# Forget term as one product of 64 rows, built on ScalarE; a gate sigmoid from exponentials and a logarithm; four modulation pieces moved ahead

## What is computed

```python
mod = c_act @ ada_w[layer] + ada_b[layer]          # shifts, scales, gates: 6 x 1024 for each layer
h = modulate(rms_norm(x, kv_norm_g), shift, scale)  # shared_kv
kvf = h @ kv_w                                      # k, v and 16 forget logits
dcum = cumsum(log_sigmoid(f_logit), axis=1)
...
qg = h @ w_qg                                       # fox_mixer, with h modulated by other vectors
q, gate = rms_norm(qg[..., :D]), sigmoid(qg[..., D:])
logits = (q @ k.T) * scale + dcum[t] - dcum[s]      # 16 heads of 64, causal
o = softmax(logits) @ v
y = (o * gate) @ w_o
```

## Time and profile before

| | |
|---|---|
| median of three runs | 1785.41 us (1780.71 to 1785.68) |
| profiled execution: its own time, its span | 1787.7 us, 1785.9 us |
| PE busy | 1735.7 us, 97% of the span |
| DVE, ACT busy | 1141.9 us (64%), 897.9 us (50%) |
| mean granted TensorE clock | 0.987 of full |
| DMA | 363.45 MB, mean 204 GB/s |

### The profile page before, as it was taken

The page is one execution under the profiler, slowest core; times in us unless marked ns, Lnnn a source line. Parts: engine busy times, 40 slices in busy tenths (PEclk is TensorE's granted clock), DMA queues, the critical chain, the costliest instruction groups (busy, mean ns, idle before and its releaser), DMA issues.

```text
span 1785.9 us, 22395 instructions
## 1 busy us (share of the span) xinstructions
PE 1735.7 (97%) x9104; PEld 1444.5 (81%) x9104; DVE 1141.9 (64%) x1588; ACT 897.9 (50%) x1282; POOL 7.7 (0%) x21
## 2 busy tenths in 40 slices
PE   8999999999999999999999989999999999999998
PEld 5898788888867888888888867888888889778887
DVE  3779978779666754565547967554655556675553
ACT  4645644465657444554444566444544445574432
POOL 0000000000000000000000000000000000000000
PEclk9999999999989999999999999999999999999999
DMA  9957677866615665555555324545554556345451
GB/s 385 379 227 295 238 306 294 305 244 230 258 72 189 235 222 179 200 191 181 176 201 183 119 71 177 183 171 188 204 186 175 192 205 224 111 149 181 170 195 47
DMA packets 54984, 363.45 MB, mean 204 GB/s; under 512 B 5841, under 2 KB 9041, under 8 KB 14690
## 3 DMA queue, kind: packets, MB, share of 16 engines
q1 hardware_dynamic: 53122, 351.47, 53.6%
q0 software_dynamic: 1760, 10.56, 1.5%
HBM read 360.96 MB, written 1.05 MB: 203 GB/s over the span
## 4 chain that ended last, share of the span: by engine, by line
PE 79%; DVE 10%; ACT 2%; issue 1%; DMA 0%; DVEq 0%; ACTq 0%
PE pp L633 76%; DVE low L1892 3%; PE pp L908 2%; DVE raw L1905 1%; PE pp L840 1%; DVE hf L2036 1%; PE pp L985 1%; ACT wh L1350 1%; DVE hl L1892 0%; DVE Sb L2187 0%; DVE sc L2288 0%; DVE x L1895 0%; DVE tb L1892 0%; DVE h L1892 0%; DVE top L2285 0%
## 5 line engine op out<-in xcount | busy, mean ns | idle before, releaser
L1892 DVE TENSOR_TENSOR low<-raw,wh 128x2048 fp32r<-128x2048 f32 (+3 forms) x346 | 638.8, 1861 | 367.9 <-ACT wh L1350 367.7
L1350 ACT ACTIVATE wh<-raw 128x2048 fp32r<-128x2048 f32 (+3 forms) x352 | 537.2, 1544 | 417.5 <-PE pp L633 288.1
L633 PE MATMUL pp<-wh,hh 128*128 128x512 f32 x1312 | 522.7, 398 | 7.4 <-ACT hh L1617 2.2
L633 PE MATMUL pp<-low,hh 128*128 128x512 f32 x1312 | 514.0, 392 | 1.8 <-DVE low L1892 1.6
L633 PE MATMUL pp<-wh,hl 128*128 128x512 f32 x1312 | 507.2, 392 | 3.7 <-DVE hl L1892 3.7
L633 PEld LDWEIGHTS pp<-wh,hh 128*128 128x128 f32 x1312 | 247.6, 189 | 65.3 <-issue 13.9
L633 PEld LDWEIGHTS pp<-wh,hl 128*128 128x128 f32 x1312 | 247.5, 189 | 57.6 <-DVE hl L1892 5.0
L633 PEld LDWEIGHTS pp<-low,hh 128*128 128x128 f32 x1312 | 248.0, 189 | 51.8 <-DVE low L1892 3.5
L633 PE MATMUL pp<-wh,hidh 128*128 128x512 f32 x592 | 232.0, 392 | 0.0
L633 PE MATMUL pp<-low,hidh 128*128 128x512 f32 x592 | 230.6, 389 | 0.3 <-DVE low L1892 0.3
L633 PE MATMUL pp<-wh,hidl 128*128 128x512 f32 x592 | 230.6, 389 | 0.0
(11 more groups left out here) (226 smaller groups left out, 1190.7 us busy)
## 6 DMA issues: line engine op xcount, KB each, us to landing
raw<-in_w SPq DMA_DIRECT2D x300, 1024.0 KB, 4.8
raw<-in_w SPq DMA_DIRECT2D x24, 768.0 KB, 4.3
raw<-in_w SPq DMA_DIRECT2D x13, 512.0 KB, 19.1
firstw<-in_w SPq DMA_DIRECT2D x6, 1024.0 KB, 14.8
gain<-in_w POOLq DMA_DIRECT2D x6, 512.0 KB, 4.8
bT<-in_rel POOLq DMA_DIRECT2D x1, 2048.0 KB, 12.0
cst<-in_csts POOLq DMA_DIRECT2D x1, 1029.0 KB, 7.2
xT<-in_xT SPq DMA_DIRECT2D x1, 1024.0 KB, 5.8
```

What stands on the lines that cost most here:

```text
L633: return e.matmul(out, lhsT, rhs, start=start, stop=stop, skip_group_check=True)
L1350: q.then_inc(e.activation(wh[j % NW][:, c], raw_of(i, kt * n)[:, c], ACT.Copy), s_wh, (j, part))
L1892: return e.tensor_tensor(out, a, b, op)
```

## The change

Four edits in one. First, the forget term: `dcum` is no longer split into two tiles; rows 32 to 63 and 96 to 127 of `dH` are overwritten with the rest (the rows hold copies of the same 16 logits), so hi and rest stand below each other in 64 rows, and each unit adds one fp32r product of 64 rows. The left side and eight right sides are built on ACT. Second, `h3` is built on ACT (`third_h`), in 16 activations of 128x128, and the transposes' PSUM banks are given back by ACT. Third, sigmoid(x) = exp(min(x,0) - ln(1 + exp(-|x|))): ACT does Abs, Exp, Ln and a last Exp, DVE does `gate_min` (out of the PSUM) and `gate_less`. No other table set is loaded. The PSUM area is free when the second `gate_min` has read. In the fill of attention, a step without work is added before `head_norm("q1")` and one before "own". Fourth, `marks`: by the 52nd piece 36 and not 32 ada pieces are mixed in, so that four more lie in the first feed-forward and none between `kv_v` and the second `kv_v`.

```diff
-    marks = [(0, 0), (6, 4), (18, 12), (20, 12), (52, 32), (56, 32), (72, 44), (78, 44), (88, 48)]
+    marks = [(0, 0), (6, 4), (18, 12), (20, 12), (52, 36), (61, 36), (70, 44), (78, 44), (88, 48)]
@@ tensor: s_h3 is signalled by third_h on ACT
+            if hv == 3:
+                return s_h3, ("hf", 3, m, c)
@@ tensor: attention, scores
-                            rr = slice(32 * (h % 4), 32 * (h % 4) + 32)
-                            for i in range(2):
-                                ins = mm(s_r.of((kind, "s", u["u"], s))[:, 0:nk], dL[i][rr, 128 * u["qb"]:128 * u["qb"] + 128],
-                                         dR[i][h // 4][rr, 0:nk], False, i == 1)
+                            rr = u["rows"]
+                            ins = mm(s_r.of((kind, "s", u["u"], s))[:, 0:nk], dL[rr, 128 * u["qb"]:128 * u["qb"] + 128],
+                                     dR[h // 2][rr, 0:nk], False, True)
@@ tensor: fill
                 yield from group("q1", 0, h(3), (s_side, ("qk", "q1")), fillp)
                 yield
+                yield
                 head_norm("q1", t_r)
                 yield "second"
-                yield from group("gate1", 0, h(3), (s_gate, ("gate", 1)), fillp)
+                yield from group("gate1", 0, h(3), (s_side, ("gate_min", 1, 1)), fillp)
+                yield
                 yield "own"
@@ scalar
-                q.then_inc(e.activation(gT[:, 4 * g:4 * g + 4, :], ring.of((("gate", "gate1")[g], 0)).tiles, ACT.Sigmoid),
-                           s_gate, ("gate", g))
-                log_tables()
+            def gate_log(g, ring):
+                ...
+                for n in range(2):
+                    t = slice(2 * n, 2 * n + 2)
+                    q.then_inc(e.activation(a[:, t, :], ring.of((("gate", "gate1")[g], 0)).tiles[:, t, :], ACT.Abs),
+                               s_sideact, ("gate_abs", g, n))
+                q.wait_ge(s_sideact, ("gate_abs", g, 1))
+                q.then_inc(e.activation(a, a, ACT.Exp, scale=-1.0), s_sideact, ("gate_exp", g))
+                q.wait_ge(s_sideact, ("gate_exp", g))
+                q.then_inc(e.activation(a, a, ACT.Ln, bias=1.0), s_sideact, ("gate_log", g))
+            def gate_sigmoid(g):
+                o = gT[:, 4 * g:4 * g + 4, :]
+                q.wait_ge(s_side, ("gate_less", g))
+                q.then_inc(e.activation(o, o, ACT.Exp), s_gate, ("gate", g))
@@ scalar: fill (gate_sigmoid(0) in q1's fourth step)
                 head_squares("q1", fillp)
                 yield
+                yield
                 head_roots("q1", t_r)
...
-                gate_sigmoid(1, fillp)
+                gate_log(1, fillp)
                 waiting("fox", 4, gT)
+                yield
                 yield "own"
+                gate_sigmoid(1)
@@ scalar: main order
+            def third_h(m):
+                ...                 # 2 x 4 activations 128x128, PSUM -> h3, scale and bias per row
+            def forget_sides():
+                ...                 # waits for the two "dD"
+                e.activation(dL[:, :], dH[:, :], ACT.Identity, bias=fc[:, 1:2], scale=fc[:, 0:1])
+                for j in range(8):
+                    ins = e.activation(dR[j][:, :], dH[:, :], ACT.Identity, bias=fc[:, 10 + j:11 + j], scale=fc[:, 2 + j:3 + j])
+                q.then_inc(ins, s_sideact, "dR")
             for g in range(2):
-                ahead.group("kv_k", g)
+                ahead.group("kv_k", g, between=lambda: third_h(g))
...
             values(("vv", 1), "kv_v", 1, vv[:, :, 512:1024])
-            ahead.group("q", 0)
+            forget_sides()
+            ahead.group("q", 0, upto=1)
             head_squares("q")
             ahead.first("gate", 0)
             head_roots("q")
-            gate_sigmoid(0, pairs)
+            gate_log(0, pairs)
@@ vector
+            def gate_min(g, ring):
+                ...                 # 2 x min(x, 0), PSUM -> gT, 128x512, each after its gate_abs
+            def gate_less(g):
+                ...                 # gT = gT - log, 128x1024
@@ vector: fill (gate_less(0) in q1's third step)
                 yield from ahead.steps("gate1", 0, "T")
+                gate_min(1, fillp)
                 for tile in range(4):
                     lo_of(4, tile, gT[:, tile, :])
+                yield
+                gate_less(1)
                 yield "own"
@@ vector: main order
-            ahead.group("kv_k", 0, between=lambda: h_parts(3, 0, *inputs_of("q")))
+            ahead.group("kv_k", 0)
-            ahead.group("kv_k", 1, between=lambda: h_parts(3, 1, *inputs_of("q")))
+            ahead.group("kv_k", 1)
-            q.then_inc(tt(dD[:, :], dT[:, :], dH[:, :], ALU.subtract), s_side, "dD")
-            q.wait_ge(s_side, "dD")
-            for i, d in enumerate((dH, dD)):
-                e.tensor_scalar(dL[i][:, :], d[:, :], fc[:, 0:1], fc[:, 1:2], ALU.mult, ALU.add)
-                for j in range(4):
-                    ins = e.tensor_scalar(dR[i][j][:, :], d[:, :], fc[:, 2 + j:3 + j], fc[:, 6 + j:7 + j], ALU.mult, ALU.add)
+            for r in (slice(32, 64), slice(96, 128)):
+                q.then_inc(tt(dH[r, :], dT[r, :], dH[r, :], ALU.subtract), s_side, ("dD", r.start))
...
             head_scale("q", qg, qT[:, 0:4, :])
+            gate_min(0, pairs)
```

More of the change, by code:

```diff
@@ L175, in constants @@
     z = np.zeros((128, 128))
-    forget = np.zeros((128, 10))
+    forget = np.zeros((128, 18))
     forget[:, 0] = p % 32 < 16
     forget[:, 1] = p % 32 >= 16
-    for j in range(4):
-        for g in range(4):
-            forget[32 * g + 16 + 4 * j + g, 2 + j] = -1.0
-            forget[32 * g + 4 * j + g, 6 + j] = 1.0
+    for j in range(8):
+        for g in range(2):
+            for part in range(2):
+                forget[64 * g + 32 * part + 16 + 2 * j + g, 2 + j] = -1.0
+                forget[64 * g + 32 * part + 2 * j + g, 10 + j] = 1.0
     made = {"ident": np.eye(128),
@@ L352, in build @@
         lf = [place(f"lf{i}", [128, T], F32, big + 34816 + 1024 * i) for i in range(3)]
[L353 to L356 removed]
+        dH = place("dH", [128, T], F32R, big + 34816)
+        dL = place("dL", [128, T], F32R, big + 33792)
+        dR = [place(f"dR{j}", [128, T], F32R, big + 36864 + 1024 * j) for j in range(8)]
         aq = place("aq", [128, 4, T], F32, big)
@@ L1170, in tensor_program @@
             whole("q", 0, h(3), (s_side, ("qk", "q")))
-            whole("gate", 0, h(3), (s_gate, ("gate", 0)), between=lambda: head_norm("q"))
+            whole("gate", 0, h(3), (s_side, ("gate_min", 0, 1)), between=lambda: head_norm("q"))
             into_attention()
@@ L1646, in fox_fill @@
             def fox_fill():
-                yield from ahead.steps("q1", 0, "T")
+                for n, _ in enumerate(ahead.steps("q1", 0, "T")):
+                    if n == 3:
+                        gate_sigmoid(0)
+                    yield
                 head_squares("q1", fillp)
+                yield
                 yield
@@ L1809, in scalar_program @@
             q.then_inc(e.activation(lf[1][:, :], lf[1][:, :], ACT.Ln, bias=1.0), s_sideact, "lf_ln")
+            def third_h(m):
+                acols, shift = inputs_of("q")
+                q.wait_ge(s_side, ("der", "q"))
+                q.wait_ge(s_mod, ("sec", PRE["q"][3]))
+                for c in range(2):
+                    q.wait_ge(s_aux, ("hT", 3, m, c))
+                    for i in range(4):
+                        k = 4 * c + i
+                        ins = e.activation(h3[:, m, k, :], misc.of(("hT", 3, m, c))[:, 128 * i:128 * i + 128], ACT.Identity,
+                                           bias=shift[:, k:k + 1], scale=acols[:, k:k + 1])
+                    q.then_inc(ins, s_h3, ("hf", 3, m, c))
+            def forget_sides():
+                fc = C("forget")
+                for r in (32, 96):
+                    q.wait_ge(s_side, ("dD", r))
+                e.activation(dL[:, :], dH[:, :], ACT.Identity, bias=fc[:, 1:2], scale=fc[:, 0:1])
+                for j in range(8):
+                    ins = e.activation(dR[j][:, :], dH[:, :], ACT.Identity, bias=fc[:, 10 + j:11 + j], scale=fc[:, 2 + j:3 + j])
+                q.then_inc(ins, s_sideact, "dR")
             for g in range(2):
-                ahead.group("kv_k", g)
+                ahead.group("kv_k", g, between=lambda: third_h(g))
                 head_squares("kv_k%d" % g)
@@ L2224, in lo_of @@
                 s_lo.at["h", hv, tile, 0] = s_lo.n
+            def gate_min(g, ring):
+                for n in range(2):
+                    t = slice(2 * n, 2 * n + 2)
+                    q.wait_ge(s_sideact, ("gate_abs", g, n))
+                    q.then_inc(e.tensor_scalar(gT[:, 4 * g + 2 * n:4 * g + 2 * n + 2, :],
+                                               ring.of((("gate", "gate1")[g], 0)).tiles[:, t, :], 0.0, None, ALU.min),
+                               s_side, ("gate_min", g, n))
+            def gate_less(g):
```

(10 more changed lines are left out.)

17 lines of the change are left out of this document (7 added, 10 removed).

## The result

Median 1781.03 us (1777.31 to 1784.3, 20 runs) against 1783.56 (1780.59 to 1787.85, 20 runs) of the kernel before: ratio 0.9983, 95% interval [0.9975, 0.999]. The change gains about 3 us, not the 9.1 forecast. That is less than the 0.3% that the prediction called "faster"; the time lies inside the range given, and between the forecast and rival (a). It stands nearest to rival (b)'s 1781.5, but by chance: (b)'s mechanism, that `q` waits as before, did not come.

The account below looks back on a forecast made before the run. PE, busy 97% of the span, was taken as the bound; the terms -2.5 - 2.7 - 2.7 + 0.9 - 1.9 + 0.7 - 0.9 sum to -9.1 us, giving a median of 1776.3 us, range 1771.5 to 1784.

Parts of the forecast that it names:

- rival (a): Clock falls behind a longer first-gate gap, q1's norm gains nothing, forget products show only 1.5 us: 1782.4 us; chance 0.12.
- rival (b): DVE isn't what holds PE: ACT is late and q waits as before; 1781.5 us; chance 0.07.
- DVE's queue before q: Before q, relieving DVE cuts PE's idle 3.28 us to 0.75 (-2.5 us); the clock holds behind it (-2.7 us).
- The same work on ACT: Third states and forget sides moved to ACT before q and gate are hidden there: 0 us.
- Forget products: In attention, 32 of 64 forget products go, saving PE time in 16 steps: -2.7 us, bounds -1 to -4.8.
- Rival (d): One forget product of 64 rows costs as much as two of 32, so that term goes: 1779.0 us; chance 0.07.
- Four ada pieces in the first feed-forward: 9.8 us more for DVE in the first feed-forward (217 to 375 us) is covered by slack: 0 us.
- Rival (c): Pieces come late in the first feed-forward, so the kernel is slower: +3.7 us, 1789 us; chance 0.08.
- q1's norm: In attention, the empty step puts products into the waits at q1's norm: -1.9 us, bounds 0 to -3.3.
- Gates: New gate chain lengthens PE's waits: first gate before q1 +0.9 us, second gate before o +0.7 us.
- A piece that lands earlier: In attention, o's third piece lands earlier by the new list, removing PE's 0.94 us wait at 510.22: -0.9 us.

Follow-up runs that it names:

- e7: The kernel before with one forget product of 64 rows and the new list of ada pieces, nothing else; 1776.51 us, ratio 0.9952.
- e5: The kernel before with the third states on ACT alone; 1778.31 us, ratio 0.9962.
- e1: The changed kernel with the list of ada pieces as before; 1781.12 us, ratio 0.9986.
- e13: The changed kernel with Sigmoid, without the empty step before q1's norm, and with the list of before; 1778.54 us, ratio 0.9969.
- e8: The changed kernel with Sigmoid and without the empty step before q1's norm; the one before "own" stays; 1778.30 us, ratio 0.9957.
- e2: The changed kernel without the empty step before q1's norm; the one before "own" stays; 1779.18 us, ratio 0.9970.
- e11: The kernel before with the new gate (exponentials and a logarithm) alone; 1785.07 us, ratio 1.0003.
- e3: The changed kernel with Sigmoid and its table loads back, both empty steps kept; 1777.03 us, ratio 0.9965.
- e4: The kernel before with the 64-row forget product alone, its sides built on DVE, the old list; 1784.64 us, ratio 1.0001.

## Why the prediction was right or wrong

**DVE's queue before q, -2.5 and -2.7: right.** The gap is 0.81 (0.75 forecast), released by ACT's `hh` as said; seven groups of four take 0.48 each from 435.78 on, and the stage is 4.6 us shorter for 5.2; a new 0.63 us before attention's first product, for the scaled `qT`, is part of what is missing. `hl` came at 435.12 in time. The margin was far larger than needed (18 us for 3): e7 reached the same gap with the four ada pieces' 9.8 us, and e5 came within 0.25 us of it with the `h` passes' 5.4. What I missed is that the list was not needed for it.

**The same work on ACT, 0: right.** ACT in the kernel after, before q and behind it:

```profile
413.88 2.90 ACT L1842 ACTIVATE h<-pp,mod,der 128x128 f32<-128x128 f32 x8 [3.25 <-PE pp L843]
...
434.46 1.15 ACT L1435 ACTIVATE hh<-h 128x512 fp32r<-128x512 f32 x2 [2.31 <-PE pp L636]
...
436.96 4.04 ACT L1852 ACTIVATE dR<-dH,cst 128x256 fp32r<-128x256 f32 x8
```

A half of `third_h` takes 2.90 us (3 forecast), the eight right sides 4.04 and the left one 0.60, 4.6 for the 3 forecast; all of it was hidden.

**Forget products, -2.7: mechanism right, size too small, and not free to be had.** The tile's row after, against the earlier trace rows:

```profile
L636 PE MATMUL pp<-dR,dL x32: 302/382/772, 461.1 to 527.8; 64*128 64x128 f32 x16, 64*128 64x256 f32 x16
```

From the first `kT,qT` product of a step to the first `hh` product it takes 0.75 us (465.29 to 466.04), where it took 1.06 (468.21 to 469.27): 0.31 for the 0.2 forecast; at 128 columns 0.49 for 0.79. Sixteen times 0.31 are 4.9 us, a little over the term's far bound (4.8); by the sums of work it is 4.7. The 0.43 us of four products of 32 rows had become 0.40 for two of 64 rows (465.64 to 466.04), so there the products themselves gave almost nothing (at 128 columns 0.37 and 0.24, so 0.13 of the 0.31); the time went between `kT,qT` (64 rows) and the first forget product, 0.63 us before (468.21 to 468.84) and 0.35 now that both have 64 rows. So most of the saving is that of the change from 64 to 32 rows (0.28 us at 256 columns, 0.18 at 128), for which my step took the 0.1 us of the change to 128 rows behind it; that one is still there (466.04 to 466.61, 0.57). The Trainium skill, TensorEngine Tiling (Array Packing), Key Properties, says that a change of the tiling mode drains TensorE; by that rule the sum would have been 1.6 us lower, and the trace agrees with it: 0.28 us went at that place, more than the 0.1 that I had taken for it. No run changes the rows and keeps the number of products, so the two are told apart by the starts of the products alone. Rival (d) was right in its premise at 256 columns, that one product of 64 rows costs as much as two of 32, and wrong in the conclusion that nothing is saved.

**Four ada pieces in the first feed-forward, 0: the step failed.** PE is indeed without a gap from 217 to 375. The stretch that I read ended at 375, and the work behind it had no slack at all: before, `xs` stood at 374.58 on DVE and PE's transposes at 375.17. The last pieces of `dn0` land later on ACT (367.87 for 366.24), the residual starts 1.5 us later on DVE, PE waits 1.58 us and the clock goes to 0.50 behind that. Counting "three of seven places" said how dense the list is at most in the feed-forward, not what stands ahead of the residual. e1 and e13 show that the list makes this gap, since with the old list it is gone. By the start of the transposes it costs 1.5 us here, 2.3 in e7 and 2.0 in e8 (377.49 and 377.14 for 375.17). Rival (c) didn't come: the feed-forward itself has no gap.

**q1's norm, -1.9: wrong sign, and the step that failed by most.** It cost 2.3 us by the ratios of e2 and the change, whose intervals overlap, and by attention's stretch 1.6 us beside Sigmoid and 2.8 beside the new gate (the table under e8); in the trace the wait is 2.73 us at the turn with it and 2.63 at the norm without it. The step took for granted that PE has something to do in the empty step. But the empty step brings the next turn forward, and that turn's normalising wasn't ready, the less so as the steps had become shorter.

**Gates, +0.9 and +0.7: sizes.** At the first gate the wait is 0.82 for 0.32 us, +0.5; where the gate alone is changed it is the +0.9 of the forecast (1.22 for 0.32 in e11, 1.23 in e2 for 0.34 in e8). At the second, 2.90 for 2.15 before o, +0.75 for the +0.3 of the chain (2.90 in e2 for 2.46 in e8, 2.59 in e11 for 2.15: some 0.3 of it comes with the new product), and 1.40 behind it, where 0.4 was put down for `gate_less`; that wait needs the empty step too. Together 2.7 us for 1.6, by the ratios of e3 and the change about 3.2, and by attention's stretch 2.5 us without the empty step and 3.6 with it. The clock stayed at 1.00 behind the first gate, so rival (a)'s fall didn't come there. That `q1`'s norm gains nothing, (a) had right.

**A piece that lands earlier, -0.9: right, and worth more.** With the list the product's saving is visible: e4 with the old list 1.0001, e7 with the new one 0.9952, intervals far apart. Part of those 8.6 us is the hole before `q` (e7's stage to attention is 26 us for 31). In attention alone e7 took 70.29 us and e4 74.24. I had the two terms added up as if they were independent; they are not: the wait that the list removes is 0.94 us long with the old product and 3.34, 3.23 and 1.31 us with the new one (e4, e13, e1), the first two with the slower transfer.

**The clock.** The change has moved the stretches at 0.50 (the 1.2 GHz level) more than removed them: none is left at 437 and at 519, but one is at 378 behind a wait of 1.58 us, one at 481 behind 2.73, one at 491 behind 1.12, and one at 535, where only waits of 0.81, 0.27 and 0.62 us stand ahead. The prediction had the one behind the wait before o stay. In this trace it is gone behind 2.90 us; in those of e1, e2, e7 and e8 it is there behind 2.46 to 2.90. Of the 20 runs of the changed kernel the four with a mean clock of 0.992 or 0.994 took 1777.31 to 1780.44 us, the four with 0.988 or 0.989 took 1783.94 to 1784.3.

So the sum failed in its second half. Up to attention it was -5.2 and came out at -4.6 + 1.5. In attention it was -3.9 and came out at -2.2. By the stretches, product, list and the step ahead of "own" took it from 76.57 to 69.15 us (e8), -7.4 for the -3.6 forecast, 1.7 of it from less time at 0.50; the new gate and the empty step before `q1`'s norm, for which -0.3 was forecast (+1.6 - 1.9), put 5.2 back. The steps that failed are these: that an empty step fills the wait at `q1`'s norm with the next turn (-1.9 forecast, +1.6 to +2.8 measured), for that turn's normalising was not ready either; that the two gates cost 1.6, when they cost 2.5 to 3.6; and that four ada pieces in the feed-forward cost nothing, when they cost 1.5. That the total still came as near as it did is luck: the product saved almost twice its term, and the profiled clock gave 1.7. Taken away (e8), gate and empty step leave some 7.7 us of gain; e7 with fewer edits has 8.6, the forecast's size. Open is why the clock falls at 535, why the transfer in e4 and e13 is slower, and what the step ahead of "own" does.

## What to carry to other kernels

Before a saving on the bounding engine is counted, ask of each wait in the same stage whether its releaser will come sooner too: a transfer that lands when it lands, with a queue behind it, turns the saving into a longer wait (0.94 to 3.34 us here), until that one place is eased. Look at the transfer itself as well: of the 2.4 us that this wait grew by, 1.8 came from a transfer that took 6.5 us instead of 4.8. An empty step gains only when what comes next is ready. When work is moved ahead into a stretch without gaps, read the first hand-over behind the stretch, not the stretch. And time the edits of a bundle one by one: of these, third states alone gave 6.8 us and product with list 8.6, while the whole gave 3.

## What was not expected of the hardware

The time of one kernel spreads over 7 us from run to run (1777.31 to 1784.3 after, 1780.59 to 1787.85 before), more than the change is worth, and in the runs of the changed kernel it goes with the mean granted clock. The same 1 MB transfer, alone under way, took 4.6 to 4.8 us in five traces and 6.4 and 6.5 in two (e13 and e4). Going from a product of 64 rows to one of 32 held PE 0.28 us more at 256 columns and 0.18 more at 128 than staying at 64 rows. An activation with two pointer operands took 0.36 us at 128 columns (eight in 2.90) and 0.50 at 256 (eight in 4.04), where one with immediate operands takes 0.33 at 256 (four in 1.32, `hh<-gT`); the prediction had priced the forget sides by the latter, 3 us for 4.6. A Sigmoid with a table load behind it (2.3 us to the next activation's start, its own load having been made ahead) was cheaper on the path than three activations out of one table set (3.17 us).
